# Weight slabs of a hybrid decoder layer: one DMA of 4096 columns each, or four of 1024 on the same queue

## The chip, the cores and the metric

The kernel runs on one Trainium2 chip, on 8 cores at once. Each core works on one prompt sequence of the batch and 16 of the 128 sample sequences, and loads its own copy of all weights; the cores do not talk to each other. The metric is the device time in microseconds (us) of the slowest core. Each core has TensorE (PE, matmuls), VectorE (DVE), ScalarE (ACT), GpSimd (POOL) and SyncE (SP), and 16 DMA engines that all its DMA queues share. DMAs issued by POOL appear as queue q0, those of SP and ACT as q1.

## The reference

One layer on (tokens, 1024), in fp32, for a prompt of 2048 tokens after 16 learned meta tokens, and for 4 new tokens of each sample sequence:

```
h = rmsnorm(x, g_mix)
u, q, k, v, og, zr, ga, gb = split(h @ w_in)
y_a = pool_mix(u) @ w_pool_proj            # causal window means 2/4/8/16 minus the token, group map
o   = gla(q, k, v, log_sigmoid(zr @ w_gk_up + b_gk) / 16)   # 4 heads, chunked recurrence with state S
y_b = (rmsnorm_head(o) * silu(og)) @ w_gla_proj
x   = x + (sigmoid(ga) * y_a + sigmoid(gb) * y_b) @ w_out
x   = x + (silu(rmsnorm(x) @ w_gate) * (rmsnorm(x) @ w_up)) @ w_ffn_out     # inner width 2816
y   = rmsnorm(x, g_final)
```

The outputs are y for prompt and sample, the last 15 pooling inputs, and the GLA states.

## The kernel before

A core goes through the layer twice, in passes of 1024 prompt tokens, 8 units of 128 tokens each; the first pass also carries a unit S of 80 rows (64 sample tokens and the 16 meta tokens). Activations that feed a matmul are bf16 and lie transposed (hT: 8 blocks of 128 model dimensions by tokens). In the first pass PE transposes them (`norm_b`, L403); later an SP DMA transpose does it (`xpose`, L412, through `norm_t`), and so for keT and for the GLA output.

All large weights come as slabs of [128, 4096]. The source in memory is fp32, the slab in SBUF is bf16; the DMA that loads it converts, and such a DMA is issued from POOL. Four ring buffers (ring0 to ring3, NRING = 4) hold slabs. The list `slabs` (L339) fixes their order: 12 of kind 'a' a pass (w_a: the parts of w_in, the two branch projections, w_out), 15 of kind 'f' and 2 of kind 'g' (w_f, w_f2: FFN; a 'g' slab has 3072 columns), and once 'ssb', the sample states. `slab_topup` (L346) issues the next slab as soon as the one four before it has been released; `slab_release` (L371) is called in program order behind the last matmul that reads a slab, so that the issue waits on POOL for that matmul. While `limit` is small, in the first 35 us, `more_slab` lets one more slab in at a written place among the norm steps.

POOL works in order. Besides slab issues it loads x in the first pass (`load_x`) and the small constants, and it does two small steps for each norm: `rpow` (L331) adds epsilon (L335) and raises to the power -0.5 (L319). These give the `stat` columns that DVE needs for `napply` (L396), and the `gst` columns for the GLA output (`sR`, `sC`, L788 to L803). So a slab issue stands in POOL's queue between such steps.

A class `Trk` orders everything by semaphores. `T.dma` (L177) takes a list of (destination, source) pairs: it waits once on its engine, issues one DMA for each pair, and records one write event whose semaphore value is the total behind the last pair. A reader of the buffer waits for that value.

In the second pass the slabs around the waits named below are: slab a9 (second half of gate b), issued with a10 when PE leaves the branch projection w_pool_proj; and f2 (6 FFN blocks: the last 2 of group 0), issued with g0 when the output projection (`oproj`, L1013) has read its two slabs. GLA steps (`gla`, L708) are merged between the dense matmuls of q/k for block B, pool mix and gates (`dense1`, L950); the first of them reads keTM, which two DMA transposes of keT write.

Of the kernel before, what the change touches and what calls it, by code (L numbers as in the profile page):

```python
# [197 lines left out]
def build_program():  # L198
# [91 lines left out]
    T = Trk(nc, es)  # L290
# [55 lines left out]
    def slab_topup():  # L346
        while sl['issued'] < min(len(slabs), sl['limit']):
            j = sl['issued']
            if j - NRING >= 0 and not sl['done'][j - NRING]:
                break  # L350
            i = j % NRING
            kind, x = slabs[j]
            if kind == 'a':
                dst, src = ring[i][:, :], w_a[x]
            elif kind == 'f':
                dst, src = ring[i][:, :], w_f[x]
            elif kind == 'g':
                dst, src = ring[i][:, 0:3072], w_f2[x]
            else:
                dst, src = ring[i][:, :], sgla.rearrange("p s c v -> p (s c v)")  # L360
            T.dma('pool', f'd_ring{i}', [(dst, src)], writes=[dst])
            sl['issued'] += 1

    def next_slab(kind, x):
        slab_topup()
        j = sl['next']; sl['next'] += 1
        assert slabs[j] == (kind, x), (slabs[j], kind, x)
        assert j < sl['issued']
        return j, ring[j % NRING]

    def slab_release(j):  # L371
        sl['done'][j] = True
        slab_topup()
# [64 lines left out]
    def more_slab():  # L438
        sl['limit'] += 1
        slab_topup()  # L440
# [7 lines left out]
    for u in range(2, 4):  # L448
        load_x(0, u, 'pool')
    T.dma('sp', 'd_gm', [(gmix_bc[32 * i:32 * i + 1, 512 * i:512 * i + 512], g_mix[0:1, 512 * i:512 * i + 512]) for i in range(2)],  # L450
          writes=[gmix_bc[0:64, :]])
# [44 lines left out]
    for p in range(2):  # L496
# [511 lines left out]
        if has_s:  # L1008
            for i2 in range(2):
                T.dma('sp', f'd_sin{i2}', [(Sall[:, i2 * 2048:(i2 + 1) * 2048], sgla[:, 8 * i2:8 * i2 + 8].rearrange("p s c v -> p (s c v)"))],  # L1010
                      writes=[Sall[:, i2 * 2048:(i2 + 1) * 2048]])
# [301 lines left out]
```

How the kernel before makes its waits and increments, by code:

```python
    def _wait(self, e, deps, skip=()):  # L144
        for s, v in deps.items():
            if s in skip:
                continue
            if self.waited[e].get(s, 0) < v:
                self.eng[e].wait_ge(self.sems[s], v)
                self.waited[e][s] = v
# [11 lines left out]
    def op(self, e, fns, reads=(), writes=()):  # L162
        if callable(fns):
            fns = [fns]
        reads = self._all(reads)
        writes = self._all(writes)
        deps = self._deps(reads, writes)
        own = 'E_' + e
        self._wait(e, deps, skip=(own,) if e == 'pe' else ())
        ins = None
        for f in fns:
            ins = f(self.eng[e])
        self.tot[own] += 1
        ins.then_inc(self.sems[own], 1)
        self._commit((own, self.tot[own]), reads, writes)
# [1 line left out]
    def dma(self, q, sem, pairs, reads=(), writes=(), **kw):  # L177
# [5 lines left out]
            deps[sem] = self.tot[sem]  # L183
        self._wait(q, deps)
        for (out, in_) in pairs:
            ins = self.eng[q].dma_start(out=out, in_=in_, **kw)
            self.tot[sem] += 16
            ins.then_inc(self.sems[sem], 16)
        self._commit((sem, self.tot[sem]), reads, writes)
# [1 line left out]
    def wait_all(self, e, semnames):  # L191
        for s in semnames:
            if self.tot.get(s, 0) > 0 and self.waited[e].get(s, 0) < self.tot[s]:
                self.eng[e].wait_ge(self.sems[s], self.tot[s])
                self.waited[e][s] = self.tot[s]
```

## Time and profile before

| | |
|---|---|
| median of 3 runs | 901.42 us (901.03 to 901.44) |
| profiled execution | 901.29 us; span of the slowest core (core 0) 900.2 us |
| spans of the 8 cores | 896.3 to 900.2 us, granted TensorE clock 0.998 to 0.999 |
| PE busy | 875.1 us (97%) |
| DVE, ACT, POOL busy | 438.6, 261.0, 128.3 us (49%, 29%, 14%) |
| q0 (POOL's DMAs) | 66.75 MB, 43.5% of the time of 16 engines |
| q1 (SP's and ACT's DMAs) | 32.63 MB, 15.3% |

The times of the rows are counted from the start of the span. PE is the busy engine; the other engines' busy shares alone say little, since what matters is which of them PE waits for and when. The MB of a queue are those written: a slab counts as 1 MB, while 2 MB are read for it.

### The profile page before, as it was taken

The numbers are of one execution on the slowest core, as the hardware profiler recorded it, in microseconds if no ns is written. First come the engines' busy times: TensorE is split into PE (matmuls) and PEld (weight loads), VectorE is DVE, ScalarE is ACT, GpSimd is POOL, SyncE is SP. The second block draws the span as 40 slices with busy tenths as digits, with TensorE's granted clock in tenths as the row PEclk, the third lists the DMA queues.
The fourth block names the chain that finished last, engine by engine and source line by source line (L and its number), as shares of the span: only waits on it lengthen the run. The fifth ranks groups of instructions, "written<-read, shape, count | busy, mean of one in ns | idle before, by whom it ended". The sixth has DMA issues, their size and how long they took to land.

```text
span 900.2 us, 14507 instructions; the slowest of 8 cores (896.3 to 900.2 us)
## 1 busy us (share of the span) xinstructions
PE 875.1 (97%) x4888; PEld 447.7 (50%) x4888; DVE 438.6 (49%) x715; ACT 261.0 (29%) x515; POOL 128.3 (14%) x242
## 2 busy tenths in 40 slices
PE   4999999999999999999999999999999999999996
PEld 2544566654664566456644444444444444444443
DVE  4689565657435322433267664565651331232146
ACT  4563533223322123012226614332231011101123
POOL 4535112002100000100022001120120000000002
PEclk9999999999999999999999999999999999999999
DMA  8984842749709824943695994353774844352504
GB/s 208 219 167 78 118 75 38 127 98 157 129 24 180 171 34 84 166 92 68 110 173 171 214 203 72 59 90 44 132 114 62 135 88 68 55 113 47 94 24 164
DMA packets 57116, 100.50 MB, mean 112 GB/s; under 512 B 41538, under 2 KB 42178, under 8 KB 49748
## 3 DMA queue, kind: packets, MB, share of 16 engines
q0 software_dynamic: 10336, 66.75, 43.5%
q1 hardware_dynamic: 46564, 32.63, 15.3%
q8 instruction: 41, 0.67, 0.3%
q14 instruction: 31, 0.25, 0.1%
q10 hardware_dynamic: 144, 0.20, 0.1%
HBM read 139.36 MB, written 11.53 MB: 168 GB/s over the span
## 4 chain that ended last, share of the span: by engine, by line
PE 91%; DMA 4%; DVE 2%; issue 1%; ACT 1%; POOL 0%; DVEq 0%; POOLq 0%; ACTq 0%; SPq 0%
PE ps L422 87%; DMA ring<-w_f 1%; DMA ring<-w_a 1%; DVE R L319 1%; DMA R<-R 1%; PE ps L765 1%; PE ps L829 1%; DVE R L323 1%; DMA xres<-xm 0%; PE ps L407 0%; PE ps L746 0%; PE ps L766 0%; ACT R L315 0%; PE ps L540 0%; PE ps L723 0%
## 5 line engine op out<-in xcount | busy, mean ns | idle before, releaser
L422 PE MATMUL ps<-hT,ring 128*128 128x368 bf16 (+2 forms) x2720 | 506.5, 343 | 3.0 <-DVE qeZ L323 1.1
L422 PEld LDWEIGHTS ps<-hT,ring 128*128 128x128 bf16 x2720 | 260.5, 98 | 230.3 <-issue 7.9
L313 ACT ACTIVATE sgt<-ps 128x368 f32<-128x368 f32 (+2 forms) x207 | 109.6, 530 | 432.7 <-PE ps L422 381.2
L422 PE MATMUL ps<-ring,R 128*128 128x512 bf16 (+2 forms) x1028 | 222.5, 377 | 0.0
L319 DVE TENSOR_TENSOR R<-ps,sgt 128x368 bf16<-128x368 f32 (+1 forms) x110 | 66.1, 601 | 237.1 <-PE ps L422 229.7
L422 PEld LDWEIGHTS ps<-ring,R 128*128 128x128 bf16 (+1 forms) x1028 | 101.3, 99 | 118.3 <-issue 1.2
L319 DVE TENSOR_TENSOR xres<-xres,ps 128x512 f32<-128x512 f32 (+2 forms) x103 | 69.7, 680 | 66.2 <-PE ps L422 66.0
L422 PE MATMUL ps<-R,ring 128*128 128x368 bf16 (+1 forms) x320 | 70.6, 343 | 0.0
L315 ACT ACTIVATE R<-xres 128x1024 bf16<-128x1024 f32 (+3 forms) x45 | 45.8, 1018 | 83.3 <-DVE xres L323 43.4
L186 POOL DMA_DIRECT2D ring<-w_f x34 | 18.6, 549 | 294.4 <-PE ps L422 292.8
L422 PE MATMUL ps<-ring,hT 128*128 128x512 bf16 (+1 forms) x272 | 60.3, 379 | 0.0
L335 POOL TENSOR_SCALAR stat<-stat 128x1 f32<-128x1 f32 (+1 forms) x50 | 13.6, 271 | 216.3 <-ACT R L315 214.0
L422 PEld LDWEIGHTS ps<-R,ring 128*128 128x128 bf16 x320 | 30.8, 98 | 23.5 <-issue 0.2
L422 PEld LDWEIGHTS ps<-ring,hT 128*128 128x128 bf16 (+1 forms) x272 | 26.7, 99 | 30.5 <-issue 0.3
L319 DVE TENSOR_TENSOR R<-R 128x526 f32<-128x526 f32 (+8 forms) x44 | 37.5, 854 | 6.5 <-ACT R L313 2.9
L323 DVE SCALAR_TENSOR_TENSOR sgt<-sgt,ps 128x368 f32<-128x368 f32 (+1 forms) x40 | 23.8, 595 | 24.7 <-ACT sgt L313 13.5
L323 DVE SCALAR_TENSOR_TENSOR xres<-ps,xres 128x512 f32<-128x512 f32 (+1 forms) x34 | 23.4, 688 | 19.5 <-PE ps L422 19.5
L186 POOL DMA_DIRECT2D ring<-w_a x24 | 13.9, 578 | 126.6 <-PE ps L422 118.7
L319 POOL TENSOR_TENSOR stat<-stat,negh 128x1 f32<-128x1 f32 (+1 forms) x50 | 29.3, 586 | 7.8 <-POOL stat L335 0.7
L796 DVE TENSOR_REDUCE gst<-sqb 128x4 f32<-128x512 f32 (+1 forms) x17 | 11.7, 686 | 34.6 <-ACT sqb L313 34.4
L323 DVE SCALAR_TENSOR_TENSOR R<-sgt,ps 128x368 bf16<-128x368 f32 (+1 forms) x40 | 23.6, 589 | 6.4 <-PE ps L422 3.7
L319 DVE TENSOR_TENSOR R<-R,sgt 128x368 bf16<-128x368 bf16 (+1 forms) x40 | 24.1, 602 | 4.2
(113 smaller groups left out, 443.9 us busy)
## 6 DMA issues: line engine op xcount, KB each, us to landing
ring<-w_f POOLq DMA_DIRECT2D x30, 1024.0 KB, 11.9
ring<-w_a POOLq DMA_DIRECT2D x24, 1024.0 KB, 12.3
y_p<-xres SPq DMA_DIRECT2D x15, 512.0 KB, 2.8
xres<-xp POOLq DMA_DIRECT2D x8, 512.0 KB, 12.3
R<-xp SPq DMA_DIRECT2D x8, 512.0 KB, 6.6
xres<-xp SPq DMA_DIRECT2D x8, 512.0 KB, 31.2
ring<-w_f POOLq DMA_DIRECT2D x4, 768.0 KB, 11.9
R<-sgla SPq DMA_DIRECT2D x2, 1024.0 KB, 10.6
```

The costliest lines, as they stand in the source:

```text
L186: ins = self.eng[q].dma_start(out=out, in_=in_, **kw)
L313: T.op('act', lambda e: e.activation(out=out, in_=in_, func=func, scale=scale, bias=bias), reads=rd, writes=wr)
L315: T.op('act', lambda e: e.activation(out=out, in_=in_, func=func, scale=scale, bias=bias, accum_out=accum), reads=rd, writes=wr)
L319: T.op(eng, lambda e: e.tensor_tensor(out=out, in0=a, in1=b, op=op), reads=[a, b], writes=[out])
L323: T.op('dve', lambda e: e.scalar_tensor_tensor(out=out, in0=a, scalar=s, in1=b, op0=op0, op1=op1), reads=rd, writes=[out])
L335: T.op('pool', lambda e: e.tensor_scalar(out=b, in0=a, scalar1=EPS, scalar2=None, op0=ALU.add), reads=[a], writes=[b])
L422: return [(lambda e, k=k: e.matmul(out, lhsT=lw(k), rhs=rx(k), start=(k == 0), stop=(k == K - 1))) for k in range(K)]
L765: fns.append(lambda e, h=h, hv=hv: e.matmul(bo[:, hv], lhsT=am[:, h, :], rhs=vTM[:, us, hv], start=True, stop=False))
L796: T.op('dve', lambda e: e.tensor_reduce(out=gcol[0:r, 0:4], in_=sq.rearrange("p (h v) -> p h v", h=4), op=ALU.add, axis=AX.X), reads=[sq], ...
L829: pe([(lambda e: e.matmul(banks[b][:, :], lhsT=qeZ[:, 0, 0:128], rhs=qeZ[:, 0, 0:512], start=True, stop=True)) for _ in range(n)], [qeZ[:, ...
```

## The change

Each slab's load is cut by columns into four pairs, a quarter of the columns each (1024; 768 for the 3072-column slabs), in one call of `T.dma`. The four DMAs go out one behind another on POOL's queue, on the same semaphore. The wait ahead of them, the ring buffer and the event that readers wait for stay, the latter with the value behind the fourth DMA.

```diff
--- before.py
+++ after.py
@@ -358,7 +358,8 @@
                 dst, src = ring[i][:, 0:3072], w_f2[x]
             else:
                 dst, src = ring[i][:, :], sgla.rearrange("p s c v -> p (s c v)")
-            T.dma('pool', f'd_ring{i}', [(dst, src)], writes=[dst])
+            m = dst.shape[1] // 4
+            T.dma('pool', f'd_ring{i}', [(dst[:, k * m:(k + 1) * m], src[:, k * m:(k + 1) * m]) for k in range(4)], writes=[dst])
             sl['issued'] += 1
 
     def next_slab(kind, x):
```

How POOL's instructions stand, first in the start of the first pass, from the issue of the slab with og's weights to that of the q/k slab. Before (ring2 and ring3 are the ring buffers, stat the norm columns, wpg_b the pool mixer's group map):

```order
L186 DMA ring2<-w_a 128x4096
L335 TENSOR_SCALAR stat<-stat 128x1
L319 TENSOR_TENSOR stat<-stat,negh 128x1
L186 DMA wpg_b<-w_pool_group 128x512
L335 TENSOR_SCALAR stat<-stat 128x1
L319 TENSOR_TENSOR stat<-stat,negh 128x1
L186 DMA ring3<-w_a 128x4096
```

The same place on POOL now:

```order
L186 DMA ring2<-w_a 128x1024 x4
L335 TENSOR_SCALAR stat<-stat 128x1
L319 TENSOR_TENSOR stat<-stat,negh 128x1
L186 DMA wpg_b<-w_pool_group 128x512
L335 TENSOR_SCALAR stat<-stat 128x1
L319 TENSOR_TENSOR stat<-stat,negh 128x1
L186 DMA ring3<-w_a 128x1024 x4
```

No instruction has changed its place; three more DMA issues stand ahead of a stat step at two places, and the last stat step of the first pass's input norm follows behind the second.

The second place is POOL in the second pass, behind the last stat step of the output projection: the first row after the stat steps is f2's slab, then g0 and g1. Before:

```order
L319 TENSOR_TENSOR stat<-stat,negh 128x1 [waits E_pool]
L186 DMA ring0<-w_f 128x4096 [waits d_ring0,E_pe]
L186 DMA ring1<-w_f2 128x3072 [waits d_ring1,E_pe]
L186 DMA ring2<-w_f2 128x3072 [waits d_ring2,E_pe]
L186 DMA ring3<-w_f 128x4096 [waits d_ring3,E_pe]
```

And now:

```order
L319 TENSOR_TENSOR stat<-stat,negh 128x1 [waits E_pool]
L186 DMA ring0<-w_f 128x1024 [waits d_ring0,E_pe]
L186 DMA ring0<-w_f 128x1024 x3
L186 DMA ring1<-w_f2 128x768 [waits d_ring1,E_pe]
L186 DMA ring1<-w_f2 128x768 x3
L186 DMA ring2<-w_f2 128x768 [waits d_ring2,E_pe]
```

The wait stands on the first quarter alone, and behind f2's quarters come only further slabs.

## Rows read from the trace of the kernel before

**Rows 1.** Timeline of PE, 9 to 16 us: start us, us, engine line op, tiles [idle before <-releaser].

```profile
10.04 0.69 PE L407 MATMUL ps<-ident_b,R 80*128 80x80 bf16 x8 [5.09 <-DVE R L323]
```

**Rows 2.** Timeline of PE, 530 to 690 us: all rows after idle that a DMA ended.

```profile
542.52 0.30 PE L746 MATMUL ps<-R 128*64 128x128 bf16 x4 [1.43 <-DMA R<-R]
...
604.97 1.89 PE L422 MATMUL ps<-hT,ring 128*128 128x512 bf16 x8 [0.26 <-DMA ring<-w_a]
...
678.65 3.61 PE L422 MATMUL ps<-hT,ring 128*128 128x512 bf16 x16 [1.00 <-DMA ring<-w_f]
```

**Rows 3.** Page, parts 3 and 6: packets, MB, share; then count, KB each, us to landing.

```profile
q0 software_dynamic: 10336, 66.75, 43.5%
...
ring<-w_f POOLq DMA_DIRECT2D x30, 1024.0 KB, 11.9
```

**Rows 4.** DMA view, 670 to 674 us: packets of all queues, then q0 and its share.

```profile
DMA packets 71, 0.58 MB, mean 145 GB/s; under 512 B 0, under 2 KB 0, under 8 KB 0
...
q0 software_dynamic: 71, 0.58, 97.6%
```

**Rows 5.** DMA view, landings: the first slabs issued at 594.12 and at 667.30.

```profile
ring<-w_a POOLq DMA_DIRECT2D x1, 1024.0 KB, 10.6
...
ring<-w_f POOLq DMA_DIRECT2D x1, 1024.0 KB, 11.1
```

**Rows 6.** Timeline of POOL, 3 to 33 us: slab issues and norm steps.

```profile
3.42 0.55 POOL L186 DMA_DIRECT2D ring<-w_a  x1
...
7.49 0.23 POOL L335 TENSOR_SCALAR stat<-stat 80x1 f32<-80x1 f32 x1 [2.48 <-ACT R L315]
...
26.28 0.63 POOL L186 DMA_DIRECT2D ring<-w_a  x1
...
27.34 0.46 POOL L335 TENSOR_SCALAR stat<-stat 128x1 f32<-128x1 f32 x1 [0.42 <-ACT R L315]
...
28.48 0.62 POOL L186 DMA_DIRECT2D wpg_b<-w_pool_group  x1
...
30.67 0.62 POOL L186 DMA_DIRECT2D ring<-w_a  x1
...
32.03 0.22 POOL L335 TENSOR_SCALAR stat<-stat 128x1 f32<-128x1 f32 x1 [0.73 <-ACT R L315]
```

**Rows 7.** Timeline of POOL, 594 to 668 us.

```profile
594.12 1.15 POOL L186 DMA_DIRECT2D ring<-w_a  x2 [4.00 <-PE ps L422]
...
597.49 0.23 POOL L335 TENSOR_SCALAR gst<-gst 128x4 f32<-128x4 f32 x1 [2.22 <-DVE gst L796]
...
667.30 1.16 POOL L186 DMA_DIRECT2D ring<-w_f  x2 [0.27 <-PE ps L422]
```

**Rows 8.** Timeline, 33 to 36 us: DVE's apply of the last unit, PE's transpose of it.

```profile
33.08 1.28 DVE L323 SCALAR_TENSOR_TENSOR R<-xres,stat,gmix_bc 128x1024 bf16<-128x1024 f32 x1 [0.38 <-POOL stat L319]
...
35.27 0.61 PE L407 MATMUL ps<-ident_b,R 128*128 128x128 bf16 x8
```

**Rows 9.** DMA view, 42.2 to 42.7 us, where wpg_b's narrow rows pass.

```profile
DMA packets 44, 0.08 MB, mean 164 GB/s; under 512 B 6, under 2 KB 38, under 8 KB 38
...
q0 software_dynamic: 44, 0.08, 95.3%
```

**Rows 10.** DMA view, 627.5 to 634.5 us, one slab alone.

```profile
q0 software_dynamic: 142, 1.05, 83.4%
```

**Rows 11.** DMA view, 21 to 25 us, where the x rows pass.

```profile
DMA packets 393, 1.44 MB, mean 361 GB/s; under 512 B 41, under 2 KB 41, under 8 KB 393
...
q0 software_dynamic: 393, 1.44, 101.9%
```

**Rows 12.** DMA view, 533 to 537 us: q1 while a slab is in flight.

```profile
q1 hardware_dynamic: 10, 0.00, 0.4%
```

**Rows 13.** DMA view, 538 to 540 us: q1 when that slab is done.

```profile
q1 hardware_dynamic: 974, 0.24, 193.5%
```

**Rows 14.** DMA view, 674 to 678 us: q1 beside the slab of 667.30.

```profile
q1 hardware_dynamic: 78, 0.02, 3.5%
```

## The prediction

> **What bounds the kernel now.** I read the page's first and second parts: TensorE (PE) is busy in 875.1 of 900.2 us at a granted clock of 9 tenths or more in every slice, so only what lengthens or shortens a wait of PE changes the time. Then I went through PE's timeline for rows with an idle time before them. The large ones lie in the first 16 us, where the transposes of the first three row units wait for VectorE (DVE), 5.09 us the first [rows 1]; they are over before a split weight slab could matter. Only three later waits end with a DMA, all in the second pass [rows 2]: 1.43 us at 542.52 for a DMA transpose of keT (R<-R), 0.26 us at 604.97 for a slab of w_a, and 1.00 us at 678.65 for a slab of w_f. So 2.69 us is all that faster transfers can give back directly, 0.3% of the span. All other slabs land before PE asks for them.
>
> Next I read the DMA part: q0, the GpSimd (POOL) queue, carries the slabs, one DMA of 1024 KB each, in 0.5 to 0.6 us of POOL, landing some 12 us later [rows 3]. The traffic inside one slab in flight is in [rows 4]: 71 packets in 4 us and 0.58 MB, so about 8 KB a packet: one row of 4096 bf16 values is one packet, a slab is 128 of them, 8 on each of the 16 DMA engines. The source is fp32, so the packet reads 16 KB: 17.75 packets a microsecond read 291 GB/s. At that pace a slab's data takes 7.2 us of the 10.6 and 11.1 us from issue to landing [rows 5].
>
> **The change part by part.** 59 slab loads (58 of weights, one of sample state) become 236 DMAs, 177 more. Bytes, ring buffers, semaphores and their final counts stay; the consumer still waits for all four pieces, since they are committed as one write. So a piece that lands early is of no use by itself. Three things change: POOL's time for issuing, the cost and pace of the data, and how q0 shares the engines with the SP queue (q1).
>
> *POOL's issue time.* An issue takes 0.53 us right behind another, and 0.62 first [rows 6, 7]; all DMAs of 128 rows cost this whatever their width (the 512-column wpg_b load 0.62). So I price four at 0.62 + 3 x 0.53 = 2.2 us, 1.6 more for a slab and 3.7 more for a pair. In total 59 x 1.6 = 94 us of POOL, which has 14% of the span busy; what counts is what stands behind it.
> At the start, slab 0 is issued at 3.42 and POOL's next arithmetic waits until 7.49 [rows 6]; x2 and x3 are issued 1.6 us later, but their data queue behind slab 0's anyway. Cost nothing.
> The slabs at 26.28 and 30.67 stand between the tiny rsqrt steps of the norm. At 26.28: the issues end at 28.5, the next stat step (27.34 before) starts there, 1.15 late. What is left of this when wpg_b has used POOL's idle time is small, about 0.3 us, and the slab at 30.67 starts at 31.0 and ends at 33.2. The last stat step (32.03) then starts at 33.2, 1.15 late; DVE's apply, before at 33.08, runs at 34.2 to 35.5, and PE's transpose, before at 35.27 with no wait [rows 8], starts at 35.6. Loss +0.35 us. Bounds: 0 (a narrow DMA could be issued faster) and +0.9 (if the delay at 30.67 is larger by half a step). The slack before was 35.27 - (33.08 + 1.28) = 0.91.
> In the GLA part the pair at 594.12 has a gst step behind it at 597.49 with 2.22 us idle ahead [rows 7]: 594.12 + 4.3 = 598.4, so it is 0.9 us late. It releases a DVE scaling and a transpose of ofT whose reader is the gate of block B, many matmuls on. Nothing waits; if DVE were pushed into PE's six banks it could cost the 0.9. The pair at 667.30 has only slab issues behind it (order below): free. First piece of each pair still starts at the same time.
>
> *Pace of the data.* A packet becomes 1024 columns: 4 KB read, 2 KB written, 512 a slab. The trace has no such packet, so I bound it. From below in size: between 42.2 and 42.7 us q0 moved 44 packets [rows 9], of which 6 are semaphore-size, 32 about 1 KB written and 6 of 8 KB; 95.3% of 16 engines for 0.5 us is 7.62 us. A slab in a quiet stretch takes 83.4% x 7 x 16 / 128 = 0.73 us a packet [rows 10] (the 14 semaphore packets' time counted in). Then a 1 KB packet takes (7.62 - 6 x 0.73)/32 = 0.10 us against an eighth of 0.73, 0.09. So the fixed part is about 0.01 us; 24 more packets on each engine cost 0.24 us a slab, and 0.5 with twice that. From the other side: the plain fp32 x rows, 4 KB packets and DMAs of 512 KB in a row on the same queue, read 361 GB/s [rows 11], against the slab's 291. At that pace a slab takes 5.8 us, 1.4 less. A slab's packets take 97.6% x 4 x 16 / 71 = 0.88 us at 670 [rows 4] against 0.73 quiet, so part of the time there is waiting for memory, and that hides a fixed part. I take +0.2 us a slab, between -1.4 and +0.5, nearest to the cast packets, which are the same operation.
>
> The Trainium skill, "DMA: Bandwidth & Descriptors", section "Rules for kernel authors", speaks against this change: at least 1 MiB a DMA for full bandwidth, since each has a fixed cost near 2.0 us beside bytes / 436e3. Taken in series that would add an estimated 3 x 2.0 = 6 us to every slab. The trace does not agree for DMAs queued one behind another: the x loads are half that size and q0's share is 101.9% with no gap [rows 11].
>
> *Sharing with q1.* While a slab is in flight the transposes hardly move: 10 packets of q1 in 533 to 537, then 974 in two microseconds once the slab is done [rows 12, 13]; none in 670 to 674 [rows 4], 78 in 674 to 678 [rows 14]. It looks as if a q1 packet has to wait for a q0 packet of 0.7 to 0.9 us. With packets of a quarter it should wait a quarter. The Trainium skill (same page, section "Queues, rings and completion order") says that an engine goes round its queues packet by packet, which would be this; no run here shows yet that packet size sets the turn.
> For the transpose at 542.52 this is a gain: some of its packets go before 538 instead of after. It needs to land 1.43 us sooner to free PE entirely; four times 10 packets would be little, four times the 78 of 674 to 678 about a third of the work. I take -0.7, between -1.43 and 0.
> For the slabs PE waits for it is a loss. 78 packets took 3.5% x 4 x 16 / 78 = 0.03 us each, in bulk 193.5% x 2 x 16 / 974 = 0.06. Four times as many is 234 more, 234 x 0.03 to 0.06 / 16 = 0.4 to 0.9 us. I take +0.3 for the w_f slab, where transposes are running in half the time, and +0.1 for the w_a slab, where there is one.
>
> Sum: start +0.35; transpose -0.7; slab at 604.97 +0.2 + 0.1 = +0.3 (-0.26 to +1.2); slab at 678.65 +0.2 + 0.3 = +0.5 (-1.00 to +1.4). Together +0.45, ends -2.7 and +3.9. The profiled execution took 901.29 us, so 901.74; the median before is 901.42, 0.13 above it: 901.9.
>
> **The rivals.**
> *Faster, by smaller packets.* If the quarter rows move at the x rows' pace, or the 2 us ahead of the first packet shrinks, both slab waits go and the transpose lands in time: -2.69, with the start +0.35: -2.3, so 899.1. For it: 361 against 291 GB/s. Against: the x rows have no cast, and the 1 KB cast packets show no better pace.
> *Slower, by late slabs.* The fixed part is twice what I found and q1 takes its turns four times as often: the slab at 604.97 is +1.2 and that at 678.65 +1.4 (each falls on PE in full, there is no slack), the transpose gains nothing, and the start costs 0.9: +3.5, so 904.9. It decides the sign once those two slabs together are over 1.8 us later than before. For it: both already land late; against: memory hides a fixed part.
> *Slower, by fixed costs in series.* If the 10.6 - 7.2 = 3.4 us of a slab that are not data were paid by each piece, every slab would land 10.2 us later and the two waits alone grow by 20 us: 922. [Rows 11] are against it.
> *Nothing changes because rows are cut up anyway.* 8 KB packets in [rows 4] exclude that.
>
> **How the numbers follow.** A change of less than 0.2% (1.8 us) can't be told from none here. Forecast 0.55, faster rival 0.18, late slabs 0.22, in series 0.05. My forecast lies inside 0.2% over nearly all of its own width; the faster rival is faster by 2.3 and only just passes. So 0.17 faster, 0.55 same, 0.28 slower. The range goes from the faster rival to a little above the late slabs, 899.0 to 905.5.
>
> **What would show it.** POOL: four issues of about 0.53 us a slab, and PE's transpose near 35.3 with a short wait. DMA: 512 packets a slab at 70 or so a microsecond; q1 packets during a slab several times 10 in 4 us, and the transpose at 542 landing sooner. PE: the waits at 604.97 and 678.65 at 0.5 and 1.5 us. I am wrong if a slab's time from issue to landing moves by more than 1.5 us either way, if one issue takes well over 0.6 us (a full queue holding POOL), or if PE shows a wait for a slab at a new place.

## The result, and the profile after

The changed kernel took 913.84 us (median of four) beside 901.27 us for the kernel before on the same chip: ratio 1.0124, 95% interval 1.0099 to 1.0149. It is slower, by 11 to 12 us where 0.5 was predicted, and outside the range. One of its four runs, at 996.94 us, had one die at a lower clock and is left out of the ratio, here and below; the other three took 910.01, 912.83 and 914.84 us. The profiled execution took 912.83 us; its slowest core is core 5, span 911.8 us.

The page of the changed kernel, answering to [rows 3]. Part 1, then packets, MB and share of the queues, then DMAs with their count, KB each and us to landing:

```profile
PE 878.6 (96%) x4888; PEld 449.5 (49%) x4888; DVE 439.1 (48%) x715; ACT 261.7 (29%) x515; POOL 223.2 (24%) x419
...
q0 software_dynamic: 35824, 66.76, 48.4%
...
ring<-w_f POOLq DMA_DIRECT2D x120, 256.0 KB, 9.1
ring<-w_a POOLq DMA_DIRECT2D x96, 256.0 KB, 10.9
...
xres<-xp SPq DMA_DIRECT2D x8, 512.0 KB, 23.5
```

POOL has 95 us more (94 predicted). q0 has 3.5 times the packets, and they take 13% more time (48.4% of 911.8 us against 43.5% of 900.2). SP's eight loads of x for the second pass land in 23.5 us, where the page before had 31.2. PE is busy for 3.5 us more with the same matmuls. The span of the slowest core grew by 11.6 us, so 11.6 - 3.5 = 8 us of it are new idle time. PE's timeline on core 5 shows where, answering to [rows 2] (lines are one higher than before):

```profile
30.97 0.61 PE L408 MATMUL ps<-ident_b,R 128*128 128x128 bf16 x8 [0.67 <-DVE R L323]
...
36.35 0.61 PE L408 MATMUL ps<-ident_b,R 128*128 128x128 bf16 x8 [0.86 <-DVE R L323]
...
86.40 3.61 PE L423 MATMUL ps<-hT,ring 128*128 128x512 bf16 x16 [1.67 <-DVE qeZ L323]
...
552.84 0.43 PE L747 MATMUL ps<-R 128*64 128x128 bf16 x4 [8.12 <-DMA R<-R]
...
690.04 5.34 PE L423 MATMUL ps<-hT,ring 128*128 128x512 bf16 x24 [0.71 <-DMA ring<-w_f]
```

The wait for the keT transpose, 1.43 us in [rows 2], is 8.12. By core it is 3.1, 9.1, 3.7, 4.1, 3.8, 8.1, 2.1 and 3.7 us (before: none to 1.4), and cores 1 and 5 have the longest spans. The times at which POOL issues slabs that PE has just released give the same account as milestones. From core 0 before to core 5 after (core 5 was 0.6 us ahead of core 0 at the first line before the change, 59.94, so against itself it is late by 1.7 there, and by 0.6 more than the table says in all lines down to 527.39):

| slab issue, before | after | late by | what is new since the line above |
|---|---|---|---|
| 60.51 | 61.63 | 1.1 | waits at 31 and 36 us |
| 93.45 | 95.22 | 1.8 | 0.6 more at 86 us (1.08 before) |
| 151.47 | 154.59 | 3.1 | low clock near 98 us |
| 527.39 | 531.01 | 3.6 | 0.35 for a slab at 169.74 |
| 568.74 | 580.83 | 12.1 | keT wait +6.7; low clock +1.8 |
| 836.48 | 847.87 | 11.4 | slab waits of 605 and 679 us gone or shorter |

The low clock is in the table of windows: length, busy us (count) of PE, PEld, DVE, ACT and POOL, granted clock, DMA share, GB/s. Core 5 before, then after:

```profile
550.00:565.00 15.00, 15.00 (x86) 7.24 (x84) 9.52 (x22) 5.32 (x12) 2.72 (x5) 1.00 0.13 27
```

```profile
550.00:565.00 15.00, 12.16 (x62) 5.86 (x63) 4.42 (x12) 7.51 (x14) 1.28 (x2) 0.71 0.65 75
```

A mean of 0.71 over 15 us is some 8.7 us at half (1.2 GHz) and the rest at 2.4 GHz. PE was idle for 8.12 us until 552.84, and the granted clock fell in the last part of that wait (0.84 from 545 to 550, 0.50 from 550 to 555). The matmuls behind the wait show it: four at L747 take 0.43 us, before 0.30.

Why the transpose is late is in the DMA view. First the traffic from 498 to 528 us, when three slabs are in flight beside the x loads. Core 5 before, then after (packets, MB, share):

```profile
q0 software_dynamic: 426, 3.06, 63.8%
q1 hardware_dynamic: 916, 3.34, 35.7%
```

```profile
q0 software_dynamic: 1380, 2.51, 57.9%
q1 hardware_dynamic: 1224, 4.33, 46.0%
```

The engines are full in both. But q0 moves less than before, q1 more. While a slab and the x loads are both in flight, the two queues pass nearly the same number of packets in either kernel, whatever their size. Core 5 before, 498 to 504 us, then after, 507 to 520 us:

```profile
q0 software_dynamic: 90, 0.70, 76.6%
q1 hardware_dynamic: 93, 0.36, 22.2%
```

```profile
q0 software_dynamic: 532, 0.97, 53.7%
q1 hardware_dynamic: 531, 1.94, 47.5%
```

So slab a5, issued in this stretch (at 513.02 before, from 517.20 on now), lands late. Before, the whole slab took 14.5 us. Now its last quarter, issued at 518.8, takes 22.5 (DMA view of 513 to 514 us before, of 519 to 520 after, core 5):

```profile
ring<-w_a POOLq DMA_DIRECT2D x1, 1024.0 KB, 14.5
```

```profile
ring<-w_a POOLq DMA_DIRECT2D x1, 256.0 KB, 22.5
```

Before, a5 lands 0.7 us after the next slab, a6, is issued (526.84); now it lands some 10 us after (531.01), and a6's data end late in turn. The two keT transposes are issued 5.6 us behind a6 in both. In the first 4 us they move almost nothing in either kernel: no packet of q1 before, 20 now. The next 4 us decide. Before (536.4 to 540.4 us, core 5) q0 is nearly done, and the data of both transposes pass (0.13 MB each, about 512 packets of 256 B); their landing is 7.5 us after the issue:

```profile
q1 hardware_dynamic: 1088, 0.26, 47.3%
q0 software_dynamic: 34, 0.15, 17.8%
```

Now (540.6 to 544.6) they run beside slab data, and both crawl; the two that PE waits for land 13.3 us after their issue (median):

```profile
DMA packets 625, 0.49 MB, mean 124 GB/s; under 512 B 441, under 2 KB 441, under 8 KB 624
...
q1 hardware_dynamic: 416, 0.10, 72.1%
q0 software_dynamic: 208, 0.37, 64.1%
```

A q1 packet now takes 72.1% x 4 x 16 / 416 = 0.11 us, before 0.03.

### The profile page after: what moved, and what is told of

It reads as the page before. It is cut to its first block, busy times and chain, and to the rows that moved or that the text cites. A ratio compares the mean times of both kernels' runs of the same rounds, so it can differ in the third digit from the quotient of the medians.

```text
span 911.8 us, 14684 instructions; the slowest of 8 cores (901.5 to 911.8 us)
## 1 busy us (share of the span) xinstructions
PE 878.6 (96%) x4888; PEld 449.5 (49%) x4888; DVE 439.1 (48%) x715; ACT 261.7 (29%) x515; POOL 223.2 (24%) x419
## 3 DMA queue, kind: packets, MB, share of 16 engines
q0 software_dynamic: 35824, 66.76, 48.4%
## 4 chain that ended last, share of the span: by engine, by line
PE 85%; DMA 6%; DVE 4%; POOL 2%; issue 2%; ACT 1%; DVEq 0%; ACTq 0%; POOLq 0%; SPq 0%
PE ps L423 81%; DVE R L319 3%; DMA xres<-xp 2%; DMA R<-R 2%; DMA ring<-w_a 1%; DMA ring<-w_f 1%; POOL ring L186 1%; PE ps L658 1%; DVE R L323 1%; PE ps L766 1%; PE ps L747 0%; PE ps L767 0%; ACT R L313 0%; DVE R L551 0%; PE ps L724 0%
## 5 line engine op out<-in xcount | busy, mean ns | idle before, releaser
L186 POOL DMA_DIRECT2D ring<-w_f x136 | 72.8, 567 | 256.8 <-PE ps L423 254.3
L186 POOL DMA_DIRECT2D ring<-w_a x96 | 52.1, 568 | 116.4 <-PE ps L423 107.7
L423 PEld LDWEIGHTS ps<-R,ring 128*128 128x128 bf16 x320 | 30.8, 98 | 23.5 <-issue 0.2
## 6 DMA issues: line engine op xcount, KB each, us to landing
xres<-xp SPq DMA_DIRECT2D x8, 512.0 KB, 23.5
```

What stands on the lines that cost most here:

```text
L186: ins = self.eng[q].dma_start(out=out, in_=in_, **kw)
L423: return [(lambda e, k=k: e.matmul(out, lhsT=lw(k), rhs=rx(k), start=(k == 0), stop=(k == K - 1))) for k in range(K)]
```

## The experiments

In the list of slabs, numbers 0 to 3 are the first four, and 30 to 36 begin the second pass (a3, a0, a2, a1, a4, a5, a6). Ratios are to the kernel before on the same chip, with 95% intervals; edits are against the changed kernel unless said. Line numbers move by 1 to 4 with them.

**Packet size or number of DMAs.** Four DMAs of 32 rows each keep the 8 KB packets:

```diff
-            T.dma(... [(dst[:, k * m:(k + 1) * m], src[:, k * m:(k + 1) * m]) for k in range(4)], ...)
+            T.dma(... [(dst[32 * k:32 * k + 32], src[32 * k:32 * k + 32]) for k in range(4)], ...)
```

> Four DMAs a slab, but cut by rows: 32 partitions of all 4096 columns each. Packets are 8 KB as before, 128 a slab; the number of issues and completions is that of the change. Theory T (packet size makes the wait at the first GLA unit): that wait is 0.3 to 1.5 us as before the change, time 902 to 904 us with only the issue cost at the start. Rival N (four DMAs and four completions a slab are what costs): wait over 3 us, time over 908 us.

Two DMAs with the small packets (each takes every second block of 1024 columns):

```diff
+            d4, s4 = [x.rearrange("p (b a n) -> p a b n", a=2, b=2) for x in (dst, src)]
+            T.dma('pool', f'd_ring{i}', [(d4[:, a], s4[:, a]) for a in range(2)], writes=[dst])
```

> Two DMAs a slab, each of blocks 0 and 2 or 1 and 3 of 1024 columns: packets of 2 KB written, 512 a slab, with half the issues of the change. Theory T: the wait for the keT transposes is 2 to 9 us as after the change, time 907 to 912 us (the start loses less). Rival N (number of DMAs): half of the change's loss or less, 903 to 906 us, with a wait under 3 us.

Measured: rows 1.0040 [1.0024, 1.0056], two small 1.0184 [1.0148, 1.0221]. The keT wait is at most 2.3 us by core with rows and 3.0 to 13.2 with the two. Timeline of PE, core 5 of the rows, then core 1 of the two:

```profile
545.58 0.30 PE L746 MATMUL ps<-R 128*64 128x128 bf16 x4 [1.70 <-DMA R<-R]
```

```profile
557.97 0.42 PE L747 MATMUL ps<-R 128*64 128x128 bf16 x4 [13.24 <-DMA R<-R]
```

Packet size makes the long keT wait; the number of DMAs does not. With rows q0 moves 3.10 MB in 498 to 528 us (core 5), as before. Of the rows' 0.4% (3.6 us) most is POOL's issue time: 2.0 us at the start and 0.6 at 84 us, both below. The two small DMAs lose more than expected, and more than the four quarters, with half the issues; the cause of that is open.

**Which slabs.** Three kernels quarter disjoint sets that together are all 59, and two more ask about a6 alone. The edit is the number of pieces:

```diff
+            nq = 4 if j < 4 else 1              # start only
+            nq = 4 if j in range(32, 37) else 1 # the five that meet the x loads and keT
+            nq = 1 if j < 4 or 32 <= j <= 36 else 4  # the other 50
+            nq = 4 if j == 36 else 1            # only a6
+            nq = 4 if j != 36 else 1            # all but a6
```

> Quarters only for the first four slabs of the first pass (a0, a3, a2, a1). What POOL's issues cost at the start, alone: PE's two waits of 0.6 to 0.9 us at about 31 and 36 us, and nothing else; plus 1.0 to 1.8 us, 902 to 904 us. If it is under 0.5 us, something after the start takes the delay up.

> Quarters only for five slabs of the second pass (a0 excepted: a2, a1, a4, a5, a6), all in the full stretch. B: this alone gives nearly the whole loss, wait 3 to 10 us, 906 to 912 us. If per-packet cost or issue time over all slabs is what counts, under 903 us.

> The complement of two earlier kernels: whole are the first four slabs and the five of the second pass's start (a2, a1, a4, a5, a6), the other 50 are quarters. If quarters cost something wherever PE waits for a slab soon after its issue (a9, f2 of the second pass), the ratio is 1.002 to 1.004 with waits of 1 to 3 us at f2 and at a9 or behind it, and the keT wait is at most 2 us, as in the kernel before. If the loss needs quarters in the first pass too (a backlog carried over), the keT wait is large here as well. If the two places alone carried the loss, the ratio is 1.000.

> The kernel before with one slab of 59 in quarters: a6 of the second pass, the one in flight beside the keT transposes. Theory T: this alone brings the wait to 2 us or more on most cores, 903 to 909 us. Rival B (backlog: the slabs before it, slowed by sharing with SP's x loads, push a6 and the transposes together): the wait is as before the change, 0.3 to 1.5 us, 901 to 902 us.

> All slabs in quarters but a6 of the second pass, the one whose data meets the keT transposes, in one DMA. B without mixing (a6 is late, whatever its packets): wait 3 us or more, 907 us or more. B with mixing (late, and then 2 KB packets and transposes slow each other): the 8 KB packets of a6 hold the transposes off and then let them go, wait 2 to 4 us, 904 to 908 us.

| quartered | ratio | keT wait by core |
|---|---|---|
| first four | 1.0022 [1.0012, 1.0031] | up to 1.0 us, as before |
| five, 32 to 36 | 1.0080 [1.0049, 1.0110] | 2.4 to 11.1 us |
| the other 50 | 1.0056 [1.0042, 1.0070] | 1.2 to 2.6 us |
| only a6 | 1.0007 [0.9998, 1.0017] | 0.2 to 2.3 us |
| all but a6 | 1.0153 [1.0123, 1.0182] | 1.2 to 12.8 us |

Timeline of PE, core 0 of the five, then core 7 of all but a6:

```profile
551.88 0.42 PE L748 MATMUL ps<-R 128*64 128x128 bf16 x4 [11.09 <-DMA R<-R]
```

```profile
557.62 0.42 PE L748 MATMUL ps<-R 128*64 128x128 bf16 x4 [12.83 <-DMA R<-R]
```

Five of 59 slabs carry two thirds of the loss. The packet size of the slab that runs beside the transposes (a6) is neither needed nor enough for a long wait: alone it adds about 1 us to the keT wait (none to 1.4 before), between the two theories. The other 50 cost more than the 1.002 to 1.004 expected, and they lengthen the keT wait a little too. The three disjoint sets add to 1.58% where all together cost 1.24%. The traces fit that: core 5 of the changed kernel, which waited 8 us at keT, has none for a slab near 605 us and one of 0.71 us at 690.04. Core 3 of the other 50 shows those later waits, which [rows 2] had at 0.26 and 1.00 us:

```profile
607.96 1.89 PE L424 MATMUL ps<-hT,ring 128*128 128x512 bf16 x8 [1.20 <-DMA ring<-w_a]
...
682.65 7.67 PE L424 MATMUL ps<-hT,ring 128*128 128x512 bf16 x27 [2.00 <-DMA ring<-w_f]
```

**The start.** In the kernel that quarters the first four, POOL and PE on core 0 read:

```profile
26.06 2.23 POOL L186 DMA_DIRECT2D ring<-w_a  x4
...
28.36 0.22 POOL L335 TENSOR_SCALAR stat<-stat 128x1 f32<-128x1 f32 x1
...
29.97 0.80 POOL L335 TENSOR_SCALAR stat<-stat 128x1 f32<-128x1 f32 x1
...
31.46 2.22 POOL L186 DMA_DIRECT2D ring<-w_a  x4
...
33.75 0.22 POOL L335 TENSOR_SCALAR stat<-stat 128x1 f32<-128x1 f32 x1
```

```profile
30.84 0.61 PE L409 MATMUL ps<-ident_b,R 128*128 128x128 bf16 x8 [0.65 <-DVE R L323]
...
36.23 0.61 PE L409 MATMUL ps<-ident_b,R 128*128 128x128 bf16 x8 [0.86 <-DVE R L323]
```

Four issues take 2.2 us, as priced. But each of the two late stat steps is a wait of its own (1.5 us together), and the kernel loses 0.22%, 2.0 us. The low clock near 98 us belongs here too. In the profiles of the nine kernels that cut the first four slabs, 19 of 72 cores have a mean granted clock below 1.00 from 92 to 112 us (0.91 for core 5 of the changed kernel); in the seven that do not, 1 of 56. On core 1 of this kernel it is 0.50 from 97 to 99 us, behind the same wait of 1.17 us that core 0 passes at 1.00. How a delay at 31 to 36 us leads to it is open.

**Who takes the engines from whom.** SP's eight x loads moved behind the q/k matmuls of block B, in the changed kernel and in the kernel before:

```diff
-            for u in range(8):
-                load_x(1, u)
...
+            if not has_s:
+                for u in range(8):
+                    load_x(1, u)
```

> All slabs in quarters, but SP's eight x loads of the second pass (4 MB) are issued 45 us later, behind the keT transposes. Theory B (backlog: in the full stretch 490 to 545 us the quarters let the x loads past, so a5 and a6 end late and meet the transposes): slabs land in some 10 to 12 us there, the wait at the first GLA unit is under 1.5 us, time 902 to 905 us. Rival T (2 KB packets of any slab beside transposes are enough): wait over 3 us, over 908 us.

> The kernel before with the same later x loads. B: the wait of 0.3 to 1.9 us for keT shrinks; 899.5 to 902 us. T says the same up to 1 us. A new wait could stand at the w_a slab of 604.97 or at gate b, where the loads now pass: then 902 to 905 us.

And the x loads left in place but cut to 1 KB packets (plain fp32, four DMAs of 256 columns):

```diff
-                load_x(1, u)
+                T.dma('sp', f'd_sp{u}', [(xres[:, u, k * 256:(k + 1) * 256], xp[...][:, k * 256:(k + 1) * 256]) for k in range(4)], writes=[xres[:, u, :]])
```

> The changed kernel with SP's x loads of the second pass cut by columns too, four DMAs of 256 columns, 1 KB packets. Theory P (the DMA engines take q0 and q1 in turn by packets, so the ratio of packet sizes sets who gets through): the ratio is back to that before the change, q0 writes about 3.1 MB between 498 and 528 us as before the change and not 2.5 to 2.6, a5 lands in 16 us or less, the keT wait is under 2.5 us, 904 to 908 us with the waits for slabs and the start left. Rival C (the quarters' own cost on the engines makes the backlog): q0 gets no more than 2.7 MB and the wait is as in the changed kernel.

Measured: late x loads 1.0050 [1.0030, 1.0070] in the changed kernel, 0.9995 [0.9984, 1.0006] in the one before; x in quarters 1.0103 [1.0081, 1.0124]. With late x loads the keT wait is at most 0.73 us on any core, and the quarters of a4 and a5 land in 7.4 us (median, core 5). With x in quarters, 498 to 528 us on core 5:

```profile
q0 software_dynamic: 1851, 3.37, 74.5%
q1 hardware_dynamic: 2299, 2.29, 30.6%
```

q0 has its bytes back (2.51 to 3.37 MB) for one reason, that the other queue's packets became smaller; where both are in flight (503 to 508 us) it is 291 packets of q0 to 290 of q1. This confirms that here the two queues share the engines by packets, not bytes, and it excludes that the slabs' small packets are late by their own pace alone. a5's quarters land in 11.8 us (median). The keT wait falls from 2.1 to 9.1 us to 0.4 to 4.0, not to nothing and not below the 2.5 expected: in 541 to 547 us q1 then has 2655 packets in 1.25 MB, so its own x loads have not ended when the transposes come.

The Trainium skill states this sharing: by "DMA: Bandwidth & Descriptors", section "Queues, rings and completion order", an engine goes round its queues and takes a packet from each. Between slabs and x loads the counts agree, at three pairs of packet sizes (90 to 93, 532 to 531, 291 to 290). For the transposes they do not: in their first 4 us 20 of their packets passed beside 372 of q0 (core 5, after).

What the late x loads leave is on core 6:

```profile
606.94 1.89 PE L423 MATMUL ps<-hT,ring 128*128 128x512 bf16 x8 [1.14 <-DMA ring<-w_a]
682.53 7.83 PE L423 MATMUL ps<-hT,ring 128*128 128x512 bf16 x22 [2.91 <-DMA ring<-w_f]
```

**Whether a6's data must run beside the transposes.** A first try moved the release in front of a6 behind the q/k matmuls in the program (`slab_release(j_og)`):

> All slabs in quarters, but in the second pass the slab a6 is issued 14 us later, behind the q/k matmuls of block B, so that no slab is in flight when the two keT transposes of block A run. Theory T (turn-taking: quarter-size packets mix with the transposes' 256 B packets, both crawl, and PE waits 2 to 9 us at the first GLA unit, then runs below the full clock): that wait goes to under 1 us, the low-clock stretch behind it goes too, and the time is 902 to 905 us. Rival S (every slab is simply slower, the transposes only show it): still over 908 us. Rival Q (SP's x loads, which are late too, hold the transposes): the wait stays over 3 us.

Measured 1.0131 [1.0116, 1.0146], keT waits of 3.1 to 10.7 us. It tests nothing: POOL waits only for the semaphore of PE's last read, and issued a6 at 531.26 (core 2; 531.01 on core 5 of the changed kernel). Its worth is a second measurement of the change. So a6 was really held: with the release moved in the same way, by a read of keT's block B, which makes POOL wait for DVE's write of it; in the changed kernel and in the kernel before:

```diff
+            rd = [keT[:, 1, 512:1024]] if j == 36 else []
+            T.dma('pool', f'd_ring{i}', [...], reads=rd, writes=[dst])
```

> The changed kernel with the slab a6 of the second pass really held back: its first quarter waits for DVE's last write of block B's keT, some 10 us later than before (an edit of the release alone, e1, had not moved it). P with mixing: block A's keT transposes meet only the end of a5, the wait at the first GLA unit falls under 3 us on every core, 903 to 908 us. If a5's backlog alone makes the wait, it stays at 2 to 9 us and 910 us or more.

> The kernel before with a6 held in the same way, as a candidate to beat it. The 1.4 us wait for the keT transposes goes; a6 and a7 are loaded one behind the other, a6 needed only 20 us later: 899.5 to 901 us beside 901.4. If the R<-ofb transposes behind them are starved instead, no gain.

Measured 1.0051 [1.0033, 1.0069] and 0.9997 [0.9988, 1.0006]. The keT wait is below 0.25 us on all cores and the clock 1.00 from 540 to 560. The first 4 us of the transposes, core 5 of the changed kernel with a6 held:

```profile
q1 hardware_dynamic: 1074, 0.26, 31.4%
q0 software_dynamic: 7, 0.01, 1.7%
R<-R SPq DMA_TRANSPOSE x2, 3.3
```

With 2 KB packets throughout, a transpose lands in 3.3 us if there is room. So the keT wait needs two things: a backlog from the shared stretch (late x loads remove it) and a further slab behind it (holding a6 removes that). Either repair gives back about 0.7%.

**Do the parts add.** Both repairs in the changed kernel: the first four slabs whole and a6 held.

```diff
+            nq = 1 if j < 4 else 4
```

> The changed kernel with the first four slabs whole again and slab a6 of the second pass held until keT's block B is written: the two repairs together. If the loss is three separate parts that add (start 0.22%, keT wait with its low clock 0.7 to 0.8%, later slabs at a9 and f2 0.2 to 0.3%), the ratio to the kernel before is 1.002 to 1.004, the waits near 31 and 36 us and at keT are gone, and those near 608 us (1 to 2 us) and 680 us (1.3 to 3 us) remain. If the start's delay was only absorbed by other waits, the ratio stays at 1.005. If all of it comes from something spread over the whole kernel (traffic slowing PE), it stays above 1.005 too.

Measured 1.0033 [1.0020, 1.0046], as three separate parts give. What is left is the slabs of 604 and 679 us (none to 2.2 us by core), and 0.6 us at 84 us. With rows of 8 KB packets the wait near 680 us is 0.9 to 1.5 us where there is one, about as before (1.0 to 1.3), so what makes these slabs later is the packet size too, and not the number of DMAs. Timeline of PE on core 0 and on core 7:

```profile
84.20 3.62 PE L426 MATMUL ps<-hT,ring 128*128 128x512 bf16 x16 [1.67 <-DVE qeZ L323]
```

```profile
603.86 1.89 PE L426 MATMUL ps<-hT,ring 128*128 128x512 bf16 x8 [0.75 <-DMA ring<-w_a]
678.72 11.60 PE L426 MATMUL ps<-hT,ring 128*128 128x512 bf16 x53 [2.18 <-DMA ring<-w_f]
```

The 0.6 at 84 (1.08 before) appears only in kernels that cut the sample-state slab, and not in the one that quarters the first four alone (1.07). POOL issues that slab in front of its own pooling steps. Core 0 before, then here:

```profile
39.88 0.62 POOL L186 DMA_DIRECT2D ring<-sgla  x1 [6.91 <-PE ps L422]
```

```profile
38.78 2.22 POOL L186 DMA_DIRECT2D ring<-sgla  x4 [6.48 <-PE ps L426]
```

No version beat the kernel before: the two that remove its keT wait (late x loads, a6 held) are at 0.9995 and 0.9997, and the wait for f2 is up to 2.2 and 1.7 us there, where it was at most 1.3.

## Why the prediction was wrong

*Which waits there are.* "All other slabs land before PE asks for them" was true, and the wrong filter. Slabs a4 and a5 are read late, so a few us did not matter to PE; but their data stood in front of the transposes PE does wait for. The saturated stretch from 490 to 545 us was never read as a stretch. The page's DMA row and x's 31.2 us to landing, 2.6 times those of a slab, showed it.

*"Sharing with q1" is the step that failed, in sign.* It priced what q1 gains from smaller turns only at two slabs (0.4 to 0.9 us), and for the keT transpose as a gain of 0.7 us. Measured: the term is 0.7 us to 8.8 us of loss, by core, against the same core before, and 0.7% to 0.8% of the time with its low clock (what holding a6, or moving the x loads, gives back). Two errors. The turns went to the x loads, 4 MB of them, not to transposes, and a5's last quarter took 22.5 us to land. And I had read [rows 12, 13] as a q1 packet waiting for one long q0 packet. It is not so: with quarter packets the transposes' first 4 us were as empty, and where the two did mix, both crawled. What the rows show is that transposes move in bulk where q0 is empty, so the end of q0's work was what to predict.

*Start, +0.35.* POOL's issue time was right to 0.1 us (2.12 to 2.23 against 2.2), and the second wait is at the transpose that was named (36.35, predicted 35.6). The 3.7 us for a pair was a slip: eight issues at those prices take 4.3, 3.2 more than two, and 4.3 to 4.4 is what is measured. The size was off: +1.5 us on PE, and 2.0 by its own kernel. The slack of 0.91 us was counted for the last stat step only. The delay behind the first, called "about 0.3 us", was 0.8: on core 0 of the kernel that quarters the first four, wpg_b is issued at 29.27 (28.48 before) and the second slab at 31.46 (30.67), and PE waits 0.65 to 0.88 us where no wait was expected. The third issue at 39.88, in front of POOL's pooling steps, was not looked at: +0.6 at 84 us.

*Slabs of 605 and 679 us, +0.3 and +0.5.* Direction right, size too small. With the keT wait removed they are up to 1.9 and 3.0 us by core (0.26 and 1.00 in [rows 2]), so the worst cores are beyond the ends given (+1.2, +1.4), and they cost 0.3% together with the 84 us wait. In the changed kernel itself they are hidden behind the keT wait (0.71 at 690.04).

*Pace of the data, +0.2 us a slab.* Mis-sized as well, at or beyond its upper bound of +0.5. The time of q0's packets rises by 50 us (48.4% of 911.8 against 43.5% of 900.2), 0.84 us a slab with waits for other traffic counted in. A quiet slab, answering to [rows 10], shows 0.5: 79.4% of 8 us (575 packets, 629 to 637 us, core 0) against 83.4% of 7. It adds to the backlog and to the later slabs, by how much was not measured apart; the larger part of the backlog are the turns, since q0's bytes come back with the x loads in quarters.

*The sum.* Its upper end, +3.9, is 0.4 too high: 0.9 + 0 + 1.2 + 1.4 = 3.5, as in the rival. Neither reaches the measured 11 to 12.

*The rivals.* "Slower, by late slabs" had the sign and one right cause (q1 takes turns four times as often) at the wrong place. Fixed costs in series are excluded: a quarter lands 9.1 us after its issue (median of the page), the last being issued 1.6 us behind the first, where a whole slab took 11.9. "I am wrong if PE shows a wait for a slab at a new place" missed too: the wait was at an old place and for a transpose. The first sign named, a slab's landing that moves by more than 1.5 us, did come, for a5.

*The low clock* was in no term. It is part of the price of a wait here. From 540 to 560 us the granted clock is 0.74 on core 5 (keT wait 8.1 us), 0.91 on core 3 (4.1), 1.00 on core 0 (3.1) and on core 3 of the kernel with the other 50 slabs quartered (2.4), and 1.00 wherever the wait is gone.

Open: why both queues crawl where transposes and slab data mix. At its worst they nearly stand. Core 7 of all but a6, 546 to 550 us, where q0's six packets are a6's, of 8 KB. The first line has the starts of packets in slices of 0.1 us:

```profile
DMA  0090040900040900003990004090004090006090
...
DMA packets 147, 0.08 MB, mean 21 GB/s; under 512 B 141, under 2 KB 141, under 8 KB 141
...
q1 hardware_dynamic: 141, 0.04, 163.8%
q0 software_dynamic: 6, 0.05, 6.5%
```

A q1 packet is 163.8% x 4 x 16 / 141 = 0.74 us there, and 31.4% x 4 x 16 / 1074 = 0.02 where a6 is held. Packets start in bursts some 0.6 us apart, about as long as one packet of a6 takes, which looks as if the transposes moved in step with a6's packets; no run tests it. The worst were found on cores whose keT wait passes 8 us, also where a6 has 8 KB packets, so a6's packet size is not their direct cause. Nor was it tested what decides when a transpose's packets begin to move beside a slab.

## What to carry to other kernels

Where two queues had work, they shared the DMA engines by packets here, so cutting one queue's rows handed its share to the queue with longer packets: before changing a packet size, find the stretches where engines are full and ask whose data will end later and what stands behind it. Price a transfer that nobody waits for by what it blocks; a DMA transpose behind a backlog cost PE up to 13 us here. And an issue costs POOL the same for 512, 1024 and 4096 columns (0.53 to 0.63 us), so cut only loads with nothing time-critical behind them on that engine.

## What the runs showed of the hardware

- A DMA transpose issued behind a casting slab load moves next to nothing in its first 4 us (0 and 20 packets, core 5). It landed in 7.5 us where the slab's data ended soon behind that, in 13.3 where they lasted, and in 3.2 to 4.2 on all cores with no further slab behind a5.
- Plain fp32 loads of SP against casting loads of POOL took packets one to one while both had work: 93 to 90 with 4 KB against 8 KB written, 531 to 532 with 4 KB against 2 KB, 290 to 291 with 1 KB against 2 KB. Over 30 us that made 3.34 to 3.06 MB, 4.33 to 2.51 and 2.29 to 3.37.
- Four DMAs of whole 8 KB rows cost 0.4% over one, most of it by POOL's issue time. The Trainium skill, "DMA: Bandwidth & Descriptors", section "Rules for kernel authors", advises at least 1 MiB a DMA for bandwidth. In the one stretch compared, four of 256 KB lost none (3.10 MB in 498 to 528 us, 3.06 before); the size that mattered here was the packet's.
- POOL's issue of 128 rows in two blocks of 1024 columns took 0.71 us, against 0.53 in one block.
- A transpose's packet took 0.02 us with free engines, 0.11 beside 2 KB slab packets, and 0.74 in the worst stretch, where the shares of the two queues add to 170% of the engines at 21 GB/s.
